# Two-block transformer on one core: exponentials one place earlier in the first attention, the last down weights fetched and split sooner

## The reference

```python
def block(args):
    q1b, q2b, start = args
    ...
    attn = probs(q1b, k1) - lam * probs(q2b, k2)     # two softmax maps, causal
    return jnp.einsum('bhqk,bhkd->bhqd', attn, v32)
...
f = jax.nn.silu(jnp.einsum('bld,df->blf', h, w_gate[l])) * jnp.einsum('bld,df->blf', h, w_up[l])
f = jnp.einsum('blf,fd->bld', f, w_down[l])
h_res = h_res + rms_norm(f, post_ffn_g[l])
```

## Time and profile before

| | |
|---|---|
| median of 3 runs | 2594.71 us (2590.66 to 2598.65) |
| the profiled execution's own time | 2594.34 us |
| its span in the profile | 2592.5 us |
| granted clock of TensorE, mean | 0.973 |
| busy: PE / DVE / ACT / POOL | 94% / 57% / 31% / 44% |
| first attention, first scores to the first product of the next stage | 309.6 to 486.3 us |
| last down step of mlp1, first matmul | 1304.1 us |
| last down step of mlp2, first matmul | 2551.8 us |

### The profile page before, as it was taken

One profiled execution on the slowest core, in us unless ns is written; L12 is line 12 of the kernel. 1 busy time (PEld: TensorE's weight loads), 2 busy tenths in 40 slices (PEclk: granted clock), 3 DMA queues, 4 the chain that ended last, 5 costly groups with the idle time before them and its releaser, 6 DMA issues.

```text
span 2592.5 us, 32813 instructions
## 1 busy us (share of the span) xinstructions
PE 2426.4 (94%) x11718; PEld 1967.5 (76%) x11718; DVE 1474.3 (57%) x2113; ACT 798.0 (31%) x1517; POOL 1150.1 (44%) x888
## 2 busy tenths in 40 slices
PE   7997877898999999999989998989989999999996
PEld 7976755686788888888768886768768888888885
DVE  5974666537456555655574311664645655555556
ACT  4231355624322222222242002552532222222222
POOL 3220040254555555665583443001745565555553
PEclk9998899898999999999999999999999999999998
DMA  5445520023111111211152113001311111111114
GB/s 144 126 130 132 169 73 1 1 81 122 37 49 49 50 59 49 60 49 49 59 181 67 45 54 106 1 1 41 123 41 58 57 53 49 49 49 50 59 49 146
DMA packets 176915, 179.29 MB, mean 69 GB/s; under 512 B 39704, under 2 KB 139544, under 8 KB 176816
## 3 DMA queue, kind: packets, MB, share of 16 engines
q1 hardware_dynamic: 171520, 164.02, 20.9%
q10 hardware_dynamic: 5296, 13.96, 1.5%
HBM read 147.46 MB, written 30.49 MB: 69 GB/s over the span
## 4 chain that ended last, share of the span: by engine, by line
PE 81%; DVE 8%; ACT 4%; issue 2%; DMA 2%; POOL 2%; SPq 0%; POOLq 0%; ACTq 0%; DVEq 0%
PE ps L267 23%; PE ps L268 23%; PE ps L269 23%; PE ps L1498 3%; PE ps L1466 3%; PE ps L1484 2%; ACT ex L1552 2%; PE ps L474 1%; DVE hbuf L425 1%; DMA msb<-ssm_lags 1%; DVE ex L1603 1%; DVE hbuf L1989 1%; PE ps L2710 1%; PE ps L456 0%; DVE hbuf L431 0%
## 5 line engine op out<-in xcount | busy, mean ns | idle before, releaser
L1989 DVE TENSOR_TENSOR hbuf<-hbuf,ps 128x1024 f32<-128x1024 f32 x320 | 390.7, 1221 | 254.0 <-PE ps L269 232.2
L267 PE MATMUL ps<-mlp_dh,mlp_fh 128*128 128x512 f32 x672 | 264.4, 393 | 12.8 <-POOL mlp_dzl L1790 10.0
L269 PE MATMUL ps<-mlp_dh,mlp_fl 128*128 128x512 f32 x672 | 263.3, 392 | 0.0
L268 PE MATMUL ps<-mlp_dl,mlp_fh 128*128 128x512 f32 x672 | 262.7, 391 | 0.0
L207 POOL TENSOR_TENSOR wgt<-raw,ones 128x512 fp32r<-128x512 f32 x76 | 86.7, 1141 | 328.3 <-PE ps L269 165.1
L1777 POOL TENSOR_TENSOR mlp_s_raw<-mlp_gh_raw,mlp_s_raw 128x512 f32<-128x512 f32 x44 | 57.1, 1299 | 284.1 <-PE ps L269 284.1
L267 PEld LDWEIGHTS ps<-mlp_dh,mlp_fh 128*128 128x128 f32 x672 | 126.6, 188 | 43.7 <-POOL mlp_dzl L1790 10.8
L269 PEld LDWEIGHTS ps<-mlp_dh,mlp_fl 128*128 128x128 f32 x672 | 126.5, 188 | 27.7
L268 PEld LDWEIGHTS ps<-mlp_dl,mlp_fh 128*128 128x128 f32 x672 | 126.7, 189 | 27.5
L1790 POOL TENSOR_TENSOR mlp_dl<-mlp_d_raw,mlp_dh 128x1024 fp32r<-128x1024 f32 x42 | 113.9, 2712 | 46.5 <-ACT mlp_dh L1966 46.5
L1484 PE MATMUL ps<-ident,ex 128*128 128x128 f32 (+1 forms) x464 | 83.0, 291 | 41.6 <-DVE ex L1603 26.6
(11 more groups left out here) (485 smaller groups left out, 6719.4 us busy)
## 6 DMA issues: line engine op xcount, KB each, us to landing
h<-hbuf SPq DMA_DIRECT2D x24, 512.0 KB, 2.9
mlp_d_raw<-in_w_down SPq DMA_DIRECT2D x21, 512.0 KB, 3.4
mlp_d_raw<-in_w_ffn_out SPq DMA_DIRECT2D x21, 512.0 KB, 3.6
raw<-in_w_in SPq DMA_DIRECT2D x40, 256.0 KB, 2.8
raw<-in_w_out SPq DMA_DIRECT2D x32, 256.0 KB, 2.7
res_b<-h SPq DMA_DIRECT2D x16, 512.0 KB, 4.4
mlp_ul<-in_w_up SPq DMA_DIRECT2D x22, 256.0 KB, 3.0
mlp_uh_raw<-in_w_up SPq DMA_DIRECT2D x22, 256.0 KB, 3.3
```

Source lines behind the costliest of these rows:

```text
L267: pe.matmul(out, lhs[0], rhs[0], start=first, stop=False, skip_group_check=over)
L268: pe.matmul(out, lhs[0], rhs[1], start=False, stop=False, skip_group_check=over)
L269: return pe.matmul(out, lhs[1], rhs[0], start=False, stop=last, skip_group_check=over)
L1989: v.tensor_tensor(self.acc[:, i, :], self.acc[:, i, :], src, ALU.add).then_inc(self.s["added"], 1)
```

## The change

1. In ACT's loop of the first attention the exponentials of item n+2 stand ahead of the evacuation of the first batch of item n+1. In DVE's loop O is done one item later, behind P: loop n does P of n+1, O of n-1, then M. P waits for O of three items before, which still reads the same sum buffers. The second attention (`maps == 1`) keeps its order.
2. The transfer of the last down weights waits for `gl` of the last window only and stands ahead of the next stage's weights on SP. ACT's copy of their high part stands right behind the silu on the gate; their buffers change places (what the names call `dzl` is now the high part, and `dzh` the remainder). In `mlp1` GpSimd splits two units of the next stage, then these weights, then two more.
3. PE's last down step begins with the parts of tile 0 and tile 1 that need only window 20, and waits for `dz` and `fz` after them.

```diff
--- before.py
+++ after.py
@@ -1559,11 +1559,13 @@
                 for b in self.steps(n):
+                    if self.maps == 2 and b == self.first[n + 1] and n + 2 < len(self.items):
+                        self.act_exp(act, n + 2)
                     if self.maps == 2 or b % 2 == 1:
                         evacuated(act, n)
-                if n + 2 < len(self.items):
+                if self.maps == 1 and n + 2 < len(self.items):
                     self.act_exp(act, n + 2)
@@ -1597,6 +1599,8 @@
                 v.wait_ge(self.s[f"exp{m}"], n + 1)
+            if n >= 3:
+                v.wait_ge(self.s["o_out"], n - 2)
             link(v.reciprocal(rl[:, n % 3, 0:2], psum_l[:, n % 3, 0:2]))
@@ -1628,6 +1632,8 @@
                     self.dve_prob(v, n + 1, link)
+                if self.maps == 2 and n >= 1:
+                    self.dve_out(v, n - 1, link)
                 if n + 2 < N and (self.maps == 1 or self.wide(n + 2)):
@@ -1635,7 +1641,8 @@
                         self.evacuate(v, nc.vector.tensor_copy, b)
-                self.dve_out(v, n, link)
+                if self.maps == 1 or n == N - 1:
+                    self.dve_out(v, n, link)
@@ -1688,8 +1695,8 @@
             self.f = [pair("f", tail + 8192), pair("fz", O_WH + 8192)]
-            self.d = [pair("d", tail + 16384), pair("dz", O_WH)]
-            self.d_raw = [at(f"{tag}_d_raw", [P, D], F32, tail + 20480), at(f"{tag}_dz_raw", [P, D], F32, O_WH + 4096)]
+            self.d = [pair("d", tail + 16384), pair("dz", O_WH)[::-1]]
+            self.d_raw = [at(f"{tag}_d_raw", [P, D], F32, tail + 20480), at(f"{tag}_dz_raw", [P, D], F32, O_WH)]
             b11, b21 = (tuple(x[:, k:k + 4, 0:HALF] for x in (xh, xl)) for k in (0, 4))
@@ -1738,7 +1745,8 @@
         def sp_last_down(self, sp):
             f = NF - 1
-            self.wait(sp, "direct", f * 2 + 2)
+            self.wait(sp, "direct", f * 2 + 1)
+            self.wait(sp, "f_hi", f * 3 - 1)
             sp.dma_start(self.d_raw[1][:, :], self.wd[:, f, :]).then_inc(self.s["raw_down"], 16)
         def freed(self, eng, n):
@@ -1786,7 +1794,7 @@
         def pool_down_lo(self, pool, f):
             z = 1 if not self.last(f) else 0
-            self.wait(pool, "f_hi", f * 3 + 2)
+            self.wait(pool, "f_hi", f * 3 + (1 if z else 2))
             nc.gpsimd.tensor_tensor(self.d[z][1][:, :], self.d_raw[z][:, :], self.d[z][0][:, :].bitcast(F32),
@@ -1824,20 +1832,39 @@
-        def pe_down_tile(self, pe, f, i, z=0, both=False):
-            if i == 0:
-                self.wait(pe, "split", self.split_of(f + 1, "down") if not both else 8 * NF + 1)
-                self.wait(pe, "f_lo", (f + 1) * 2 if not both else 2 * NF)
-            if not isinstance(f, int) or f * 8 + i >= 2:
-                self.wait(pe, "added", f * 8 + (i - 1))
+        def pe_down_part(self, pe, i, z, first, last):
             c = slice(i * P, (i + 1) * P)
                 n = slice(h * HALF, (h + 1) * HALF)
-                for z in range(2 if both else 1):
-                    mm = three(pe, ps[:, 4 + 2 * (i % 2) + h, :], (self.f[z][0][:, c], self.f[z][1][:, c]),
-                               (self.d[z][0][:, n], self.d[z][1][:, n]), z == 0, z == int(both))
-            mm.then_inc(self.s["down"], 1)
+                mm = three(pe, ps[:, 4 + 2 * (i % 2) + h, :], (self.f[z][0][:, c], self.f[z][1][:, c]),
+                           (self.d[z][0][:, n], self.d[z][1][:, n]), first, last, True)
+            return mm
+        def pe_down_tile(self, pe, f, i):
+            if i == 0:
+                self.wait(pe, "split", self.split_of(f + 1, "down"))
+                self.wait(pe, "f_lo", (f + 1) * 2)
+            if not isinstance(f, int) or f * 8 + i >= 2:
+                self.wait(pe, "added", f * 8 + (i - 1))
+            self.pe_down_part(pe, i, 0, True, True).then_inc(self.s["down"], 1)
+        def pe_down_last(self, pe, after_tile):
+            f = NF - 2
+            self.wait(pe, "split", self.split_of(f + 1, "down"))
+            self.wait(pe, "f_lo", (f + 1) * 2)
+            for i in range(NT):
+                if i != 1:
+                    for j in ((0, 1) if i == 0 else (i,)):
+                        self.wait(pe, "added", f * 8 + (j - 1))
+                        self.pe_down_part(pe, j, 0, True, False)
+                if i == 0:
+                    self.wait(pe, "split", 8 * NF + 1)
+                    self.wait(pe, "f_lo", 2 * NF)
+                self.pe_down_part(pe, i, 1, False, True).then_inc(self.s["down"], 1)
+                after_tile(pe, i)
         def pe_window(self, pe, f, odd, down=True, begun=False):
@@ -1907,9 +1934,7 @@
             self.pe_window(pe, NF - 1, 1, False)
-            for i in range(NT):
-                self.pe_down_tile(pe, NF - 2, i, both=True)
-                after_tile(pe, i)
+            self.pe_down_last(pe, after_tile)
@@ -1956,15 +1981,20 @@
                 self.act_hi(act, g, o, "gh")
+            if not more:
+                self.act_down_hi(act, f)
             self.wait(act, "taken", f * 5 + 4)
                 self.act_hi(act, g, o, "s4")
+                self.act_down_hi(act, f)
+            self.act_f_hi(act, f, 0)
+        def act_down_hi(self, act, f):
+            z = 0 if self.last(f) else 1
             self.wait(act, "raw_down", (f + 1) * 16)
-            z = 0 if more else 1
             nc.scalar.copy(self.d[z][0][:, :], self.d_raw[z][:, :]).then_inc(self.s["f_hi"], 1)
-            self.act_f_hi(act, f, 0)
         def act(self, act, middle):
@@ -2022,7 +2052,7 @@
                 c = slice(h * HALF, (h + 1) * HALF)
-                self.wait(v, "f_hi", f * 3 + (1 if h else 3))
+                self.wait(v, "f_hi", f * 3 + (3 if not h else 1 if self.last(f) else 2))
                 v.tensor_tensor(self.f[b][1][:, c], src, self.f[b][0][:, c].bitcast(F32), ALU.subtract)\
@@ -2562,9 +2592,9 @@
         mlp1.sp(sp)
+        mlp1.sp_last_down(sp)
         mlp1.freed(sp, 2)
         sp_weights(sp, N_BLOCK1, N_BLOCK1 + NRAW)
-        mlp1.sp_last_down(sp)
         mlp1.freed(sp, 4)
@@ -2609,8 +2639,9 @@
         mlp1.freed(pool, 3)
-        pool_weights(pool, N_BLOCK1, N_BLOCK1 + 4)
+        pool_weights(pool, N_BLOCK1, N_BLOCK1 + 2)
         mlp1.pool_down_lo(pool, NF - 1)
+        pool_weights(pool, N_BLOCK1 + 2, N_BLOCK1 + 4)
         mlp1.freed(pool, 5)
```

## The result

The changed kernel takes 2559.43 us by median (2554.99 to 2563.25, 4 runs), the kernel before 2595.38 (2590.66 to 2598.65, 4 runs): ratio 0.9861, 95% interval 0.9843 to 0.9878, or 32 to 41 us. The forecast was 2561, its range 2548 to 2577. The profiled execution took 2558.24, its span is 2556.4 against 2592.5, with a mean clock of 0.977 against 0.973.

A forecast was written before the change was run, and what follows sets the result against it. PE, busy 94% of the span, bounds the kernel, so only its idle or low-clock stretches can give time back. Attention 22.3, mlp1 tail 5.1 and mlp2 tail 5.8 sum to 33.2 us off 2594.34: 2561, range 2548 to 2577.

The forecast's parts named there:

- Attention, one head: First attention: 28.5 us of work plus 4.5 idle and 1.6 of clock; period 34.5 against 40.9, 6.4 us a head.
- The clock's fall at item 7's turn: First attention, item 7's first turn: the fall to the lower clock, 1.7 us lost before, was taken as gone.
- that at its scores: First attention, item 7's 1040-column scores: the fall to the lower clock was taken as staying, 1.6 us a head.
- The Trainium skill's case: First attention, weaker case: both clock falls come back in every head, 36.2 us a head, gain about 5 us smaller.
- Attention, its ends: First attention, first head to its item 7 and last from there: half of a head's gain assumed, 3.1 us.
- Tail of mlp1: Last down step of mlp1: third add 5.2 us sooner, DVE setting the pace from there; gain 5.1, bounds 3 and 6.
- Tail of mlp2: Last down step of mlp2: first add at 2551.5 against 2557.05; gain 5.8 us, bounds 4 and 6.5.
- Stronger: Rival, chance 0.19: M, P and exponentials fit under PE, clock kept; heads 31.5 to 33 us, total 2551.
- the three waits: First attention, idle left per head: item 5's turn for P 1.2, item 7's scores for O 1.5, next scores for M 1.05.
- Weaker: Rival, chance 0.16: longer wait at item 7 in the attention, both clock falls stay; heads 37.5 us, total 2573.
- slower: Rival, chance 0.04: exponentials in front drag M into the attention's evacuation path; a head about 51 us, total 2625.

The follow-up runs named there:

- e10: Changed kernel plus matmuls that compute nothing in the two waits ahead of the first attention's 1040-column scores; 2553.79 us, ratio 0.9846 to the kernel before.
- e3: The changed kernel run once more with nothing altered; 2559.49 us, ratio 0.9849 to the kernel before.
- e7: e4 plus PE doing the last product of item 4 ahead of the first turn of item 5; 2557.05 us, ratio 0.9847 to the kernel before.
- after: The changed kernel's first profile, with all three parts of the change against the kernel before; profiled execution 2558.24 us.
- e1: The kernel before with only the attention's part of the change; 2569.06 us, ratio 0.9896 to the kernel before.
- e5: Changed kernel with O back in its old place at the end of DVE's loop, exponentials still early; 2557.48 us, ratio 0.9850 to the kernel before.
- e6: Changed kernel with the old order of parts in PE's last down step, transfer, copy and split still early; 2567.42 us, ratio 0.9891 to the kernel before.
- e11: Changed kernel with O in its old place and item 4's last product ahead of item 5's first turn; 2558.34 us, ratio 0.9865 to the kernel before.
- e4: Changed kernel with DVE doing O of item 4 ahead of P of item 6, once a head; 2555.08 us, ratio 0.9839 to the kernel before.
- e8: Changed kernel plus 36 matmuls that compute nothing in the gap behind the first attention; 2560.35 us, ratio 0.9856 to the kernel before.
- e9: Changed kernel plus 26 matmuls that compute nothing in each of three gaps at the start of mlp1 and mlp2; 2552.75 us, ratio 0.9838.
- e12: Changed kernel with the fillings of e8, e9 and e10 together; 2548.52 us, ratio 0.9839 to the kernel before.

## Why the prediction came out right

*Attention, one head.* The step held, its sum and each term within 0.5 us: 28.45 us of work at full clock against 28.5, idle 4.63 against 4.5, heads 35.1, 33.1 and 34.8 apart, 34.3 on average against 34.5 (the forecast's own terms add up to 34.6). The clock's fall at item 7's turn is gone, as taken; that at its scores stayed in three of four heads. The Trainium skill's case of a gap that brings half speed back in each tile ("TensorE: Matmul & The Clock Gate", on HAM oscillation) holds here for the gap that remains, though in three of four heads and not in each, and e10 shows it from the other side: with the gap filled the fall is gone in all four heads. It did not hold for the second place, because there the gap itself was gone.

*Attention, its ends.* This term failed. The 3.1 us for the first head and the last item were half of a head's gain by assumption; from the first scores to the first 1040-column scores the profiles have 29.2 against 29.5, and from the last 1040-column scores to the first product of the next stage 26.3 against 25.7. Together nothing. The attention gave 18.8 in the profiled pair (mean of three profiles against two: 19.9), not 22.3.

*Tail of mlp1.* Right up to the third add, and wrong behind it, in two sentences: "from there DVE, with no gaps, sets the pace as before" left out that GpSimd's remaining units no longer fall into DVE's idle time (1.8 us), and "GpSimd's roots still come in time" missed a wait of 0.46. Gain 2.6 up to `xs_b` and 3.2 with the 0.6 behind it, forecast 5.1. This is read from the durations and was not tested by itself. The Trainium skill says of the port that both engines share that it is held by one at a time ("SBUF — State Buffer", two separate sides). The trace agrees (1.52 beside a unit, 0.69 alone), and the same sentence, followed 8 us further, would have given the loss.

*Tail of mlp2.* 5.76 against 5.8.

*What the sum left out.* In this pair of profiles 1.6 us of clock between the attention and mlp1 follow the change; 2.5 more at mlp1's start go with it or not from kernel to kernel, and 4.3 at two other places vary within one kernel. What is shown to belong to the change is 18.8 + 1.6 + 2.6 + 5.8 = 28.8; with the 2.5 and 0.6 that are not settled it is 31.9, against 33.2 forecast. The forecast's terms for the attention and mlp1's tail were 3.5 and 1.9 us too large, and clock that it had not counted made up for them: the total was right partly by luck. Nor do these parts reach the middle of what the whole times give, 32 to 41 us here and 34 to 44 in e3; where the other 4 us or more come from is open, since only one execution of each kernel was profiled.

*Rivals.* Stronger would have needed heads under 33; e7 and e10 reach 32.1 to 33.4, so the three waits and their falls were what stood between. Weaker and slower did not occur: the heads show no wait for evacuations that sets their end, and in the profile after one fall a head was the most.

## What to carry to other kernels

Where two engines take turns in series, look at which instruction stands in front of another in a queue for no reason of data: putting the exponentials ahead of one evacuation was worth 19 us, while O's place, which looked like part of the same repair, was worth nothing. Work that is ready put in front of a wait (two tiles' parts of the down step) was worth as much as making the awaited data earlier, or more (5.1 us of the two tails' 8.4). Before an idle gap is shortened, see what the engine's clock does behind it, and check an edit by stages and not only by the total, because a gain in one stage can come back as a loss in the next.

## What the runs showed of the hardware

TensorE's granted clock costs this kernel time behind idle gaps of about 1 to 3.5 us at many places (1.7 us at the scores, 1.6 and 2.5 at the starts of the feed-forward parts, 0.3 on a single product). The stage behind the attention took 162.7 and 162.8 us in the two profiles with the old attention, and 158.4 to 158.6 in five with the new (after, e1, e3, e5, e10), though these five began up to 7.8 us apart; but in e6, whose program up to there is the changed kernel's, it took 159.5, as in e11, and 161.1 to 161.3 in e4, e7 and e8. In e8 only matmuls that compute nothing were added upstream; whether they moved it is not settled by one profile. Such matmuls in the gap itself removed the falls (e9 at mlp1 and mlp2, e10 at the scores), with one exception in e12's first head. Whether they also steady the runs is not shown: 4 us over five runs of e9 and 1.2 over four of e10 stand against 10 over five of e3, but also against 9 over five of e12, which has all the fillings, and 5 over four of e5, which has none. What decides the level was not found.
